# Order of the weight slices, the pairs and the norm fills in the second layer's output projection of a fused two-block model

## The reference

```
h = h + concat([do, fo]) @ w_out[1]            # output projection of layer 1: 1024 x 1024 by 1024 x 1024
x = rmsnorm(h, final_gain)                     # end of the first block
h_ctx = modulate(rms_norm(ctx, g), ...)        # 256 context rows
k, v  = split(h_ctx @ w_in[:, 512:1536])       # context projection
h_lat = modulate(rms_norm(x, g), sh_a, sc_a)   # 1024 rows
proj  = h_lat @ w_in                           # token mixer begins
```

## Time and profile before

| | us |
|---|---|
| median of 3 runs (lowest, highest) | 3025.3 (3021.27, 3028.36) |
| the profiled execution, its own time | 3023.28 |
| its span, first to last instruction | 3021.5 |
| TensorE busy | 2834.5 |
| VectorE busy | 1545.5 |
| ScalarE busy | 1021.3 |
| mean granted TensorE clock | 0.977 of full speed |

### The profile page before, as it was taken

The page is one execution under the profiler, slowest core; times in us unless marked ns, Lnnn a source line. Parts: engine busy times, 40 slices in busy tenths (PEclk is TensorE's granted clock), DMA queues, the critical chain, the costliest instruction groups (busy, mean ns, idle before and its releaser), DMA issues.

```text
span 3021.5 us, 43091 instructions
## 1 busy us (share of the span) xinstructions
PE 2834.5 (94%) x17460; PEld 2423.9 (80%) x17460; DVE 1545.5 (51%) x2800; ACT 1021.3 (34%) x1960; POOL 209.5 (7%) x295
## 2 busy tenths in 40 slices
PE   6899989999898889999999898999999999999999
PEld 6777777888798777877887797888898888888887
DVE  5655555545524655654455447555436444445335
ACT  5333333323214333333233355222334222223233
POOL 1000000000101100000000106000012000000000
PEclk9999999999899999999999899999999999999999
DMA  4112221120322212222221314111332111111113
GB/s 130 39 55 60 59 55 55 55 62 29 116 61 71 54 39 63 55 59 63 73 52 43 118 55 133 49 43 46 127 100 71 49 49 49 42 49 49 49 63 133
DMA packets 205397, 198.10 MB, mean 66 GB/s; under 512 B 7286, under 2 KB 181686, under 8 KB 205198
## 3 DMA queue, kind: packets, MB, share of 16 engines
q1 hardware_dynamic: 187344, 134.27, 16.8%
q0 software_dynamic: 17856, 61.07, 5.5%
HBM read 162.73 MB, written 32.58 MB: 65 GB/s over the span
## 4 chain that ended last, share of the span: by engine, by line
PE 79%; DVE 10%; ACT 5%; issue 4%; DMA 2%; POOL 1%; SPq 0%; ACTq 0%; DVEq 0%; POOLq 0%
PE PS L595 75%; PE PS L604 4%; DVE WL L1782 1%; DVE ST L1969 1%; DMA W<-in_w_in 1%; ACT top L1362 1%; ACT WH L1214 1%; DVE AL L1825 1%; DVE AL L2152 0%; DMA R<-in_k_fg 0%; DMA TMP<-s_os 0%; DVE V L1957 0%; DVE AL L2044 0%; DVE top L1985 0%; DVE top L1982 0%
## 5 line engine op out<-in xcount | busy, mean ns | idle before, releaser
L595 PE MATMUL PS<-AH,WH 128*128 128x512 f32 (+3 forms) x2624 | 993.7, 379 | 20.5 <-DVE AL L1825 13.8
L595 PE MATMUL PS<-AL,WH 128*128 128x512 f32 (+3 forms) x2624 | 923.6, 352 | 0.0
L595 PE MATMUL PS<-AH,WL 128*128 128x512 f32 (+3 forms) x2624 | 920.9, 351 | 0.0
L595 PEld LDWEIGHTS PS<-AH,WH 128*128 128x128 f32 x2624 | 500.5, 191 | 103.2 <-issue 21.9
L595 PEld LDWEIGHTS PS<-AL,WH 128*128 128x128 f32 x2624 | 501.4, 191 | 49.7 <-issue 1.7
L595 PEld LDWEIGHTS PS<-AH,WL 128*128 128x128 f32 x2624 | 499.9, 191 | 43.0
L1782 DVE TENSOR_TENSOR WL<-W,WH 128x1024 fp32r<-128x1024 f32 x186 | 228.5, 1230 | 325.4 <-ACT WH L1214 325.2
L595 PE MATMUL PS<-WH,AH 128*128 128x256 f32 (+1 forms) x1088 | 350.7, 322 | 11.4 <-DVE WL L1782 5.3
L595 PE MATMUL PS<-WH,AL 128*128 128x256 f32 (+1 forms) x1088 | 348.7, 320 | 0.0
L595 PE MATMUL PS<-WL,AH 128*128 128x256 f32 (+1 forms) x1088 | 348.6, 320 | 0.0
L1214 ACT ACTIVATE WH<-W 128x1024 fp32r<-128x1024 f32 x186 | 195.5, 1052 | 280.4 <-PE PS L595 256.4
(11 more groups left out here) (326 smaller groups left out, 3243.8 us busy)
## 6 DMA issues: line engine op xcount, KB each, us to landing
W<-in_w_in SPq DMA_DIRECT2D x94, 512.0 KB, 7.7
W<-in_w_ada SPq DMA_DIRECT2D x48, 512.0 KB, 3.6
W<-in_w_up SPq DMA_DIRECT2D x44, 512.0 KB, 3.7
W<-in_w_out SPq DMA_DIRECT2D x24, 512.0 KB, 3.4
W<-in_w_down SPq DMA_DIRECT2D x22, 512.0 KB, 3.6
R<-s_xs POOLq DMA_DIRECT2D x16, 512.0 KB, 6.7
s_adap<-AST POOLq DMA_DIRECT2D x48, 128.0 KB, 7.9
top<-in_x SPq DMA_DIRECT2D x8, 512.0 KB, 9.3
```

The costliest lines, as they stand in the source:

```text
L595: return e.matmul(out, lhsT, rhs, start=start, stop=stop, skip_group_check=True)
```

## The change

Quarters 2 and 3 of ("out", 1) are both made pair by pair: pair 0 of quarter 2, pair 0 of quarter 3, pair 1 of quarter 2, and so on, which `tensor_out` already does for a name in PAIRED. The two slices of quarter 3 get places of their own: (3, 0) where the context's k and v are written later, (3, 1) where the modulation's gate rows stood, which have been stored by then (a wait on `gates_out` guards it). The order of the slices in PLAN becomes (0,0) (0,1) (1,0) (3,0) (1,1) (2,0) (2,1) (3,1). ScalarE and VectorE split (3, 0) at the start of quarter 0's work, (1,1) and (2,0) before the sums of quarter 1, (2,1) and (3,1) behind the context fill. All four pairs' sums of quarters 0 and 1 are finished in their own quarter. Fills 0, 1 and 2 follow pairs 1, 2 and 3, fill 3 follows quarter 0 of "ctx".

```diff
--- before.py
+++ after.py
@@ -173,6 +173,15 @@
             EXH = spot("EXH", 22304 - 20256, [128, 2, 1024])[:, :, :]
             EXL = spot("EXL", 0, [128, 2, 1024])[:, :, :]
             ALT = spot("ALT", 26914 - 26400, [128, 2])[:, :]
+
+        with ExitStack() as last_quarter:
+            def spot(name, skip):
+                last_quarter.enter_context(nc.sbuf_tensor(name + "_skip", [128, skip], F32))
+                pair = [last_quarter.enter_context(nc.sbuf_tensor(name + part, [128, 1024], F32R)) for part in "HL"]
+                return [x[:, :] for x in pair]
+
+            OXH1, OXL1 = spot("OX1", 1640)
+            OXH0, OXL0 = spot("OX0", 12704 - 3688)
         RW = 28848
         R = sb("R", [128, RW])
         at = [0]
@@ -247,7 +256,7 @@
 
 
         PLAN, WI = [], {}
-        PAIRED = {"out2": [(EXH[:, k, :], EXL[:, k, :]) for k in range(2)], }
+        PAIRED = {("out", 1): [(OXH0, OXL0), (OXH1, OXL1)], "out2": [(EXH[:, k, :], EXL[:, k, :]) for k in range(2)], }
 
         def weight(key, src, split=True):
             WI[key] = len(PLAN)
@@ -261,7 +270,7 @@
 
             order = [(q, kk) for q in range(4) for kk in range(2)]
             if name in PAIRED:
-                order = [(0, 0), (0, 1), (1, 0), (3, 0), (1, 1), (3, 1), (2, 0), (2, 1)]
+                order = [(0, 0), (0, 1), (1, 0), (3, 0), (1, 1), (3, 1), (2, 0), (2, 1)] if name != ("out", 1) else [(0, 0), (0, 1), (1, 0), (3, 0), (1, 1), (2, 0), (2, 1), (3, 1)]
             for q, kk in order:
                 weight((name, q, kk), w[512 * kk:512 * kk + 512, 256 * q:256 * q + 256]
                        .rearrange("(k p) n -> p k n", p=128))
@@ -921,9 +930,8 @@
 
         def tensor_ctx(e):
 
-            tensor_norm_fill(e, "lat", 1, [b for b in ALL if b != banks.place[("out", 1), 3, 3]])
             tensor_out(e, "ctx", [0, 128], lambda kt: [(fill_lo, ("ctxrows", 0, 7))] if kt == 0 else [], lambda q, p: (kvc_out, q),
-                       between=lambda q: tensor_norm_fill(e, "lat", q + 2) if q < 2 else None, x=(CAH, CAL))
+                       between=lambda q: tensor_norm_fill(e, "lat", 3) if q == 0 else None, x=(CAH, CAL))
 
         def tensor_states(e):
             for h in range(4):
@@ -1188,7 +1196,7 @@
             tensor_attention(e, 1)
             between = {0: lambda: tensor_mod(e), 1: lambda: tensor_fill(e, "ctxrows", XC, fill_tb)}
             tensor_out(e, ("out", 1), OUT_COLS[1], lambda kt: [(o_lo, (1, kt))], lambda q, p: (out_added, (("out", 1), q, p)),
-                       after=lambda i, among: tensor_norm_fill(e, "lat", 0, among) if i == 2 else None,
+                       after=lambda i, among: tensor_norm_fill(e, "lat", i - 1, [b for b in among if b not in (banks.place[("out", 1), 2, i], banks.place[("out", 1), 3, i])]) if i else None,
                        between=lambda q: between[q]() if q in between else None)
             tensor_ctx(e)
             tensor_mixer(e)
@@ -1429,26 +1437,23 @@
                     e.activation(JQ2, HT[:, t, 256 * q:256 * q + 256], ACT.Square, accum_out=SQ2[:, a, t, q:q + 1]).then_inc(*squared.mark((tag, q, t)))
 
             def out_last():
+
                 name = ("out", 1)
-                for q in range(4):
+                for q in range(2):
                     if q == 1:
                         ctx_stats()
                         gates()
-                    if q == 2:
-                        e.wait_ge(*mod.at(2))
-                        fill("ctxrows", [(128, 0), (128, 128)], lambda k: G1[:, 1, k:k + 1], lambda k: B1[:, 1, k:k + 1], TBc)
-                    split_to(WI[name, q, 1])
-                    if q:
-                        sum_h(q - 1, 3)
-                        sum_hf(q - 1, 2)
-                        sum_hf(q - 1, 3)
-                    if q < 3:
-                        split_to(WI[name, q + 1, 0])
-                        sum_h(q, 0)
-                        sum_h(q, 1)
-                        sum_hf(q, 0)
-                        sum_h(q, 2)
-                        sum_hf(q, 1)
+                    split_to(WI[name, 3 if q == 0 else 2, 0])
+                    for p in range(4):
+                        sum_h(q, p)
+                        if p:
+                            sum_hf(q, p - 1)
+                    sum_hf(q, 3)
+                e.wait_ge(*mod.at(2))
+                fill("ctxrows", [(128, 0), (128, 128)], lambda k: G1[:, 1, k:k + 1], lambda k: B1[:, 1, k:k + 1], TBc)
+                split_to(WI[name, 2, 1])
+                e.wait_ge(*gates_out.at(0))
+                split_to(WI[name, 3, 1])
 
             def ctx_stats():
                 e.wait_ge(*o_lo.at((1, 7)))
@@ -1495,16 +1500,15 @@
 
             def between_blocks():
                 for p in range(4):
-                    if p == 3:
-                        split_to(WI["ctx", 0, 0])
-                    sum_h(3, p)
-                    if p == 2:
-                        lat_fill(0)
+                    sum_h(2, p)
+                    sum_hf(2, p)
                     if p == 3:
                         split_to(WI["ctx", 0, 1])
+                    sum_h(3, p)
                     sum_hf(3, p)
                     lat_root(p)
-                lat_fill(1)
+                    if p:
+                        lat_fill(p - 1)
                 for q in range(4):
                     split_to(WI["ctx", q, 1] + 1)
                     b = banks.place.get(("ctx", q, 0), 0)
@@ -1513,8 +1517,8 @@
                     e.activation((KC if q < 2 else VC)[:, :, c:c + 256], o, ACT.Copy, scale=HD if q < 2 else 1.0).then_inc(*kvc_out.mark(q))
                     if q < 3:
                         split_to(WI["ctx", q + 1, 1])
-                    if q < 2:
-                        lat_fill(q + 2)
+                    if q == 0:
+                        lat_fill(3)
                     if q == 2:
                         decays()
 
@@ -2090,28 +2094,22 @@
                         e.wait_ge(*fg_in.at(0))
                     e.tensor_tensor(o, o, FG[:, c].unsqueeze(1).broadcast_to([128, 2, 256]), ALU.mult).then_inc(*fg_mul.mark((q, p)))
 
-                for q in range(4):
+                for q in range(2):
                     if q == 1:
                         inverse("ctx", RSTD[:, 16:18])
                         e.wait_ge(*rstd.at("ctx"))
                         for t in range(2):
                             e.tensor_scalar(XC[t], XC[t], RSTD[:, 16 + t:17 + t], None, ALU.mult).then_inc(*scaled.mark(("ctxrows", t)))
                         modulation()
-                    if q == 2:
-                        fill("ctxrows", [(128, 0), (128, 128)], None, TBc, CAH, CAL)
-                    split_to(WI[name, q, 1])
-                    if q:
-                        gain(q - 1, 2)
-                        gain(q - 1, 3)
-                    if q < 3:
-                        split_to(WI[name, q + 1, 0])
-                        add(q, 0)
-                        add(q, 1)
-                        gain(q, 0)
-                        add(q, 2)
-                        gain(q, 1)
-                        add(q, 3)
-                between_blocks(lambda p: add(3, p), lambda p: gain(3, p))
+                    split_to(WI[name, 3 if q == 0 else 2, 0])
+                    for p in range(4):
+                        add(q, p)
+                        if p:
+                            gain(q, p - 1)
+                    gain(q, 3)
+                fill("ctxrows", [(128, 0), (128, 128)], None, TBc, CAH, CAL)
+                split_to(WI[name, 3, 1])
+                between_blocks(add, gain)
 
             def lat_sums(p):
 
@@ -2152,33 +2150,22 @@
                     e.tensor_tensor(AL[:, k, c:c + 256], TBc[:, k % 4, :], f(AH[:, k, c:c + 256]), ALU.subtract).then_inc(*fill_lo.mark(("lat", p, k)))
 
             def between_blocks(add, gain):
-                add(0)
-                gain(0)
-                lat_sums(0)
-                add(1)
-                lat_scale(0)
-                gain(1)
-                lat_sums(1)
-                add(2)
-                lat_scale(1)
-                gain(2)
-                lat_fill(0)
-                lat_sums(2)
-                add(3)
-                split_to(WI["ctx", 0, 0])
-                gain(3)
-                split_to(WI["ctx", 0, 1])
-                lat_sums(3)
-                lat_scale(2)
-                lat_fill(1)
+                for p in range(4):
+                    for q in (2, 3):
+                        add(q, p)
+                        gain(q, p)
+                        if q == 2 and p == 3:
+                            split_to(WI["ctx", 0, 1])
+                    lat_sums(p)
+                    lat_scale(p)
+                    if p:
+                        lat_fill(p - 1)
                 for q in range(4):
                     split_to(WI["ctx", q, 1] + 1)
                     if q < 3:
                         split_to(WI["ctx", q + 1, 1])
                     if q == 0:
```

(4 more changed lines are left out.)

## The result

The kernel after took 3037.09 us (median of 4 runs, 3035.58 to 3039.59) against 3023.28 for the kernel before on the same chip: a ratio of 1.0047, 95% interval 1.0034 to 1.0059. That is slower, and by 4 us less than predicted (3041, range 3029 to 3047). Half of the 4 us is the base: the prediction added its 15.8 to 3025.3, the median of three runs, and a fourth run of 3021.08 brought it to 3023.28. The profiled execution has a span of 3037.8 us against 3021.5, so 16.3 us more in the two traces and 13.8 in the medians.

What follows compares the result with a forecast made beforehand. TensorE, busy 94% of the span, was taken to bound the kernel, so queue order matters only where it stands still. 4.0 + 6.6 + 3.9 + 1.3 = 15.8 us more gave 3041 us, range 3029 to 3047.

Steps and rivals of the forecast that it cites:

- Part 1: Quarter 0: the split of (3, 0) and eight sums ahead of the context statistics start quarter 1 later, +4.0 us.
- Part 2: First pair of quarter 2: TensorE waits for (2, 1), split behind three sums and the context fill, +6.6 us.
- ready at +11.3: First pair of quarter 2: low half of (2, 1) ready 11.3 us after the end of quarter 1.
- through at +4.6: First pair of quarter 2: TensorE done with transposes and 24 matmuls 4.6 us after the end of quarter 1.
- Part 3: Pairs and fills through "ctx": VectorE's and ScalarE's rounds outlast TensorE's, so waits total 10.0 against 6.3, counted as +3.9 us.
- The round: Per pair of quarters 2 and 3: VectorE's and ScalarE's chain takes 13.7 us, against 13.1 for TensorE.
- Part 4: Clock: one loss behind the new wait in quarter 2, none for later pauses, +1.3 us; bounds 0 and three losses.
- rival B: Whole change: quarter 0, quarter 2 and clock cost 11.9, pairs keep up and give back 6.3; +5.6, 3031 us; 12%.
- A: Start of "ctx": rounds under 13.1 us remove all 6.3 of waits, other delays hidden; -6.3, 3019 us; 8%.
- C: Splits beside GpSimd's eight scalings lose 0.8 us each, up to 4, plus two clock losses; +22, 3047 us; 15%.

Runs made afterwards that it cites:

- e7: The kernel after with only the last three of quarter 0's eight sums put behind the context statistics, gates and modulation; 3033.38 us, 1.0034 to the kernel before.
- e8: The kernel after with only the split of (3, 0) put behind quarter 0's sums, statistics and modulation; 3034.32 us, 1.0037 to the kernel before.
- e2: The kernel after with (2, 1) split ahead of the context fill, and that fill ahead of quarter 1's last three sums; 3028.47 us, 1.0020 to the kernel before.
- e12: e4 with the rounds over pairs, fills and "ctx" put back in the change's order; 3026.24 us, 1.0011 to the kernel before.
- e1: The kernel after with quarter 0's order put back as in the kernel before; 3034.06 us, 1.0036 to the kernel before.
- e4: The kernel after with quarter 0's order restored, (2, 1) split before the context fill, fill before three sums, fills' steps between sums; 3017.50 us, 0.9985 to before.
- e9: The kernel after, unedited, run again; 3039.66 us, 1.0057 to the kernel before.

## Why the prediction was right, and where it was not

**Part 1 was right: 4.0 predicted, 4.54 measured.** Its chain held step by step: load of (3, 0) 12 us (11.5 taken), split of both halves, addition, eight sums. Three of these sums carry most of it (2.89 in e7, 3.4 but for a later landing), the landing 0.86 (e8). But the sentence that the longer pause ahead of quarter 1 costs nothing more was wrong. The first 25 matmuls ran at half clock in place of 14, and quarter 1 took 25.46 us instead of 24.41.

**Part 2 was right: 6.6 predicted, 6.58 measured**, split around 24 matmuls as it was said it might be, the second part released by WL. e2 removed it and got 6.44 back. (The prediction's own terms, ready at +11.3 and through at +4.6, give 6.7.)

**Part 3: the mechanism was right, the sum was compared wrongly.** The round was 13.76 us, from one addition for quarter 2 (1818.97) to the next (1832.73), against 13.7 predicted (its terms add up to 13.6), and longer than TensorE's. VectorE's timeline of the kernel after:

```profile
1818.97 0.67 DVE L2072 TENSOR_TENSOR top<-top,PS 128x512 f32<-128x512 f32 x1
...
1828.65 4.16 DVE L2150 TENSOR_TENSOR AL<-R,AH 128x256 fp32r<-128x256 f32 x8
1832.73 0.67 DVE L2072 TENSOR_TENSOR top<-top,PS 128x512 f32<-128x512 f32 x1
```

The waits were to be 2.6, 2.3, 3.5, 0.7 and 0.9, together 10.0. e12, where quarter 0 of "ctx" kept the clock, has 2.52, 1.94, 3.49 and 0.48, and none for the last. In the kernel after they are 2.50, 0.42, 3.32 and 0.19, since 3.0 us of the same time went to matmuls at the lower clock. So the waits failed as a term by 4.3 us: most of it this, and 0.5 the wait before the mixer, which was to stay at 3.01 and is 2.50. One sign failed too: VectorE was to have no gap over 1.5 us from pair 1 on, and had three, of 2.26 (1808.16), 1.67 (1823.72) and 2.06 us (1837.28).

**Part 4 was mis-sized and misplaced.** One loss of 1.3 was predicted behind the wait in quarter 2, and none for the later pauses, because the stretch with four pauses had a clock of 1.00 before. It was 4.65: 1.05 in quarter 1, 3.0 in "ctx" and 0.6 elsewhere, and next to nothing in quarter 2, where the half clock fell inside the wait. The step that failed is that a pause's length decides where the clock falls. A pause of 2.5 us was followed by 0.70 in the kernel after and by 1.00 in e12. Another gain was missed too: the mixer's first stretch kept its clock, -1.6.

Predicted waits and clock together were +5.2, measured +4.3. In "ctx" the two errors cancelled because they are one: in a stretch where VectorE's order sets the end, a slow matmul eats the wait behind it. So far, for 3.0 us, the total was right for a reason. The rest was luck. The 1.3 that was predicted in quarter 2 and did not come was replaced by 1.05 in quarter 1, which the prediction had ruled out, and by the 0.6; and the half clock, which in e1 cost 2.4 us behind the wait for (2, 1), happened to lie in front of it. With e1's pattern the stage would have been about 175, an estimate from 172.5 + 2.4. The range of 18 us also held rival B's 3031, so the traces and not the median tell the forecast from B.

**The rivals.** A needed rounds under 13.1 and (2, 1) in time. The change had neither, and e4, which has both, has the gain that A set. B needed the pairs to keep up; they didn't. C reckoned 0.8 per split, twice the 0.4 of its row, whose two splits are one of 2.05 and one of 1.22. That price was hardly seen in this stage: in the kernel after, the six splits beside GpSimd's scalings took 1.23 to 1.25 us each, in e9, the same kernel, one of the six took 1.53, and in e12 two took 1.51 and 1.56. It turned up elsewhere, below.

The 13.8 us of the medians stand for a stage of +15.4, -1.6 behind it, and executions that spread by 4 to 8 us around their median.

## What to carry to other kernels

Bringing work forward in a queue that is written by hand costs whatever it is put in front of: here a split in front of additions, three sums in front of a statistic, a fill in front of a split. All three were a matter of order, and with them undone the same pair form is faster than the kernel before, by little (0.9985, interval up to 0.9994, and 0.9979 with the statistics first). Take losses of the clock and waits on another engine as one sum up to the next point that the other engine sets, and only the part that lies behind such a point as a price of its own. And value an edit by more than one neighbour: part 1 was worth 3.0 us in one and 5.5 in another, only because the half clock moved.
